# Query tiles in a PSUM bank of their own, with their products and rotary steps at other places of the map loop

## What is computed

```python
q, kc, vc, ks, vs, kw, vw, gt = jnp.split(h @ w_in, splits, axis=-1)
q = to_q_groups(apply_rope(q.reshape(b, seq, NSA_HEADS, hd), cos, sin), g)
kc = compress(kc, ...); vc = compress(vc, ...)
s_cmp = jnp.einsum('bgrqd,bgcd->bgrqc', q, kc) * scale
p_cmp = masked_softmax(s_cmp, cmask)
o_cmp = jnp.einsum('bgrqc,bgcd->bgrqd', p_cmp, vc)
...                      # o_slc: softmax over selected blocks; 8 blocks, top 16, so all causal ones
o_win = banded_attention(q, kw, vw, WIN_LEN)
o = gates[..., 0, None] * o_cmp + gates[..., 1, None] * o_slc + gates[..., 2, None] * o_win
return from_q_groups(o) @ w_o
```

## Time and profile before

| | before |
|---|---|
| three runs | 2541.85, 2544.45, 2547.47 us |
| median | 2544.45 us |
| the profiled execution | 2543.68 us, its span 2541.8 us |
| TensorE, matmuls busy | 2467.0 us, 97% |
| VectorE, ScalarE, GpSimd busy | 53%, 32%, 71% |
| mean granted TensorE clock | 0.993 of full speed |
| the loop over maps | from 126.8 us, scores of the last map at 328.5 us |

### The profile page before, as it was taken

How to read it: one execution, slowest core, us unless ns; L and a number is a source line. 1 busy time by engine, 2 the same in 40 slices (tenths; PEclk the granted TensorE clock), 3 DMA queues, 4 the chain that set the end, 5 groups by cost and what they waited for, 6 DMA issues and landing times.

```text
span 2541.8 us, 34039 instructions
## 1 busy us (share of the span) xinstructions
PE 2467.0 (97%) x11830; PEld 2064.1 (81%) x11830; DVE 1337.4 (53%) x2087; ACT 806.9 (32%) x1754; POOL 1797.6 (71%) x1589
## 2 busy tenths in 40 slices
PE   9999999999998999999999899999999999999997
PEld 7888888888887888888888777888878887788886
DVE  7778755665037656663177855343125455543312
ACT  3377742111028631110156533111015563311101
POOL 7867776676668876666699987666666668666664
PEclk9999999999999999999999999999999999999999
DMA  4300012323321123223222212233222221232232
GB/s 145 116 26 26 26 58 91 99 93 97 100 88 52 53 91 99 93 97 104 91 75 67 67 59 80 94 99 97 93 83 76 67 75 58 83 99 92 98 100 75
DMA packets 58117, 208.61 MB, mean 82 GB/s; under 512 B 6496, under 2 KB 6752, under 8 KB 58016
## 3 DMA queue, kind: packets, MB, share of 16 engines
q1 hardware_dynamic: 57744, 206.88, 24.9%
q10 hardware_dynamic: 272, 0.39, 0.1%
HBM read 205.09 MB, written 2.16 MB: 82 GB/s over the span
## 4 chain that ended last, share of the span: by engine, by line
PE 55%; POOL 5%; DVE 4%; ACT 2%; DMA 1%; issue 1%; ACTq 0%; DVEq 0%; SPq 0%; POOLq 0%
PE PS L897 17%; PE PS L899 17%; PE PS L898 17%; POOL WL L625 2%; POOL WH L623 1%; DVE PC L2860 1%; PE PS L1339 1%; ACT MP L2095 1%; DMA raw<-stream 1%; POOL RQ L692 0%; PE PS L1316 0%; POOL RQ L685 0%; PE PS L1317 0%; PE PS L1364 0%; POOL WH L622 0%
## 5 line engine op out<-in xcount | busy, mean ns | idle before, releaser
L625 POOL TENSOR_TENSOR WL<-raw,WH 128x1024 fp32r<-128x1024 f32 x380 | 921.8, 2426 | 31.7
L897 PE MATMUL PS<-HH,WH 128*128 128x512 f32 x2240 | 886.0, 396 | 20.8 <-DVE HL L2432 9.4
L899 PE MATMUL PS<-HH,WL 128*128 128x512 f32 x2240 | 876.6, 391 | 0.0
L898 PE MATMUL PS<-HL,WH 128*128 128x512 f32 x2240 | 876.2, 391 | 0.0
L897 PEld LDWEIGHTS PS<-HH,WH 128*128 128x128 f32 x2240 | 423.1, 189 | 116.4 <-issue 17.6
L899 PEld LDWEIGHTS PS<-HH,WL 128*128 128x128 f32 x2240 | 422.6, 189 | 89.4
L898 PEld LDWEIGHTS PS<-HL,WH 128*128 128x128 f32 x2240 | 423.1, 189 | 85.1 <-issue 1.0
L622 POOL TENSOR_TENSOR WH<-raw,SC 128x32 fp32r<-128x32 f32 x380 | 109.5, 288 | 490.4 <-DMA raw<-stream 475.1
L623 POOL TENSOR_SCALAR WH<-raw 128x992 fp32r<-128x992 f32 x380 | 407.2, 1072 | 0.0
L897 PE MATMUL PS<-GH,WH 128*128 (+1 forms) x688 | 268.7, 390 | 0.0
L898 PE MATMUL PS<-GL,WH 128*128 (+1 forms) x688 | 267.9, 389 | 0.0
(11 more groups left out here) (398 smaller groups left out, 3515.9 us busy)
## 6 DMA issues: line engine op xcount, KB each, us to landing
raw<-stream SPq DMA_DIRECT2D x380, 512.0 KB, 3.6
X<-x SPq DMA_DIRECT2D x4, 512.0 KB, 5.2
out<-X SPq DMA_DIRECT2D x8, 256.0 KB, 2.1
PR<-params SPq DMA_DIRECT2D x1, 536.0 KB, 8.5
spare_raw_nsa<-stream SPq DMA_DIRECT2D x1, 512.0 KB, 3.6
spare_raw_swa<-stream SPq DMA_DIRECT2D x1, 512.0 KB, 4.5
spare_raw_diff<-stream SPq DMA_DIRECT2D x1, 512.0 KB, 4.5
spare_raw_fox<-stream SPq DMA_DIRECT2D x1, 512.0 KB, 4.5
```

The lines of the kernel that those rows point to most:

```text
L625: pool.tensor_tensor(WL[:, w], raw[:, w], hi.bitcast(F32), ALU.subtract).then_inc(chunk_split, 1)
L897: pe.matmul(to, h, his[k], start=start and k == 0, stop=False)
L898: pe.matmul(to, h, los[k], start=False, stop=False)
L899: last = pe.matmul(to, l, his[k], start=False, stop=stop and k == n_k - 1)
```

## The change

For nsa, every query tile from 1 on goes to bank 6 (`Q_BANK`) and the compressed part of every pair to bank 7 (`CMP_BANK`), where tile 0 also goes. The first two output tiles go to banks 6 and 7 in that order. In pairs u from 1 on, the products of the query tiles move: at i = 0 the k-steps 2 and 3 of tile u+1 stand between the scores and the turn that waits (3 alone in pair 1), and steps 4 to 7 behind the compressed scores; nothing at i = 1; at i = 2 and i = 3 one k-step each of tile u+2, between the scores and the turn, the first of them behind a wait for the copy of tile u+1 out of the bank. In the same pairs the copy out of the bank moves from i = 1 to i = 0; the cosines to i = 1, ahead of the scaling of the compressed part; the addition to i = 1, behind the scaling of the map; first part, stacking and rest from i = 3 to i = 2. Pair 0 keeps its order. VectorE's order isn't touched. The waits for `c_lo` in `fill` at i = 3 and at m = 27 become waits for the copy.

```diff
--- before.py
+++ after.py
@@ -182,6 +182,7 @@
 TURN_BANK = (3, 4, 3)
 TURN_WIDTH = (512, 512, 256)
 AV_BANK = 5
+Q_BANK, CMP_BANK = 6, 7
 
 
 def proj_bank(x):
@@ -191,11 +192,13 @@
 
 def out_bank(kind, t):
 
-    return (proj_bank(t + 1) if kind == "nsa" else proj_bank(t)) if t < 2 else ((0, 1, 3, 2, 4, 5) if kind in GROUPED else (0, 1, 3, 2, 0, 1))[t - 2]
+    return proj_bank(t) if t < 2 else ((0, 1, 3, 2, 4, 5) if kind in GROUPED else (0, 1, 3, 2, 0, 1))[t - 2]
 
 
 def bank_at(kind, part, y=0):
 
+    if kind == "nsa" and part == "q":
+        return CMP_BANK if y == 0 else Q_BANK
     return proj_bank([x for x in ORDER[kind] if x[0] != "cmp"].index((part, y)))
 
 
@@ -835,22 +838,25 @@
                     split(c, c + 1)
                 for m in range(8 * per):
                     u, i = divmod(m, per)
+                    late = 1 if nsa and u == 0 else 0
                     if nsa and i == 0 and u < 7:
                         split(c + u, c + u + 1)
-                    if u < 7 and i == (2 if nsa else 0):
+                    if u < 7 and i == (1 + late if nsa else 0):
                         cosines(u + 1)
                     if nsa and i == cmp_step(u) + 1:
                         scale_cmp(u)
-                    if u < 7 and i == (2 if nsa else 0):
+                    if u < 7 and i == 0 and not nsa or late and i == 2:
                         if not nsa and m == 12:
                             out_rest(0)
                         add_sines(u + 1)
-                    if u < 7 and i == (3 if nsa else 1):
+                    if u < 7 and i == (2 + late if nsa else 1):
                         rest_q(u + 1, m)
                     if not nsa and i == 1 and u < 6:
                         split(c + u + 1, c + u + 2)
                     if nsa or i == 0:
                         scale(m)
+                    if nsa and 0 < u < 7 and i == 1:
+                        add_sines(u + 1)
                     for t in REST_AT[kind].get(m, ()) if nsa or m > 12 else ():
                         out_rest(t)
                     if not nsa and m == 15:
@@ -1099,7 +1105,7 @@
                     for t in range(QT):
                         for h in range(2):
                             g = 2 * (u % 2) + h
-                            to = PS[:, bank_at(kind, "q", u), 2 * (2 * t + h) * NCMP:2 * (2 * t + h + 1) * NCMP]
+                            to = PS[:, CMP_BANK, 2 * (2 * t + h) * NCMP:2 * (2 * t + h + 1) * NCMP]
                             qs = MQ[:, u % 2, h, t * P:(t + 1) * P]
                             last = pe.matmul(to, qs, KC[:, g].rearrange("p a n -> p (a n)"), start=True, stop=True)
                     last.then_inc(c_scores, 1)
@@ -1108,7 +1114,7 @@
 
                     pe.wait_ge(c_scaled, u + 1)
                     for t in range(QT):
-                        last = pe.transpose(PS[0:2 * NCMP, bank_at(kind, "q", u), t * P:(t + 1) * P],
+                        last = pe.transpose(PS[0:2 * NCMP, CMP_BANK, t * P:(t + 1) * P],
                                             CS[:, 2 * NCMP * t:2 * NCMP * (t + 1)], IDF[:])
                     last.then_inc(c_turned, 1)
 
@@ -1153,6 +1159,16 @@
                         pe.wait_ge(c_lo, u + 1)
                         pe.matmul(PS[:, AV_BANK], VC[:, k], PTC[:], start=False, stop=True).then_inc(m_av, 1)
 
+                def fill_ahead(m):
+
+                    u, i = divmod(m, per)
+                    if 0 < u < 6 and i == 2:
+                        pe.wait_ge(q_out[kind], u + 2)
+                    if 0 < u < 6 and i >= 2:
+                        proj("q", u + 2, i - 2, i - 1)
+                    if 0 < u < 7 and i == 0:
+                        proj("q", u + 1, 3 if u == 1 else 2, 4)
+
                 def fill(m):
 
                     u, i = divmod(m, per)
@@ -1176,18 +1192,13 @@
                         pe.wait_ge(mv_out, before("mv_out", kind) + 4)
                         proj("q", 1, 0, 4)
                         compress_out()
-                    elif u < 7 and i == 0:
-                        proj("q", u + 1, 3, 4)
-                    elif u < 7 and i == 1:
+                    elif u < 7 and i == (0 if u else 1):
                         proj("q", u + 1, 4, CT)
-                    elif 0 < u < 6 and i == 3:
-                        pe.wait_ge(c_lo, u + 1)
-                        proj("q", u + 2, 0, 3)
                     if u < 8 and i == cmp_step(u) + 2:
                         turn_cmp(u)
                     if m == 27:
 
-                        pe.wait_ge(c_lo, 7)
+                        pe.wait_ge(q_out[kind], 8)
                     if m == 31:
 
                         pe.wait_ge(c_lo, 8)
@@ -1253,6 +1264,8 @@
                 for m in range(8 * per + 2):
                     if m < 8 * per:
                         scores(m)
+                    if nsa:
+                        fill_ahead(m)
                     if 2 <= m < 8 * per and ng == 3:
                         turn(m - 2, (2,))
                     fill(m)
@@ -1263,6 +1276,7 @@
                     if m >= 2:
                         values(m - 2)
                     if nsa and m == 3:
+                        pe.wait_ge(q_out[kind], 2)
                         proj("q", 2, 0, 3)
                     if m == 1 and nsa:
                         pe.wait_ge(cmp_stored, 2)
@@ -1885,7 +1899,7 @@
                     act.wait_ge(c_turned, u + 1)
                     if u:
                         act.wait_ge(m_av, before("m_av", kind) + 2 * u)
-                    act.activation(PTC[0:HD], PS[0:HD, bank_at(kind, "q", u)], ACT.Copy).then_inc(c_hi, 1)
+                    act.activation(PTC[0:HD], PS[0:HD, CMP_BANK], ACT.Copy).then_inc(c_hi, 1)
 
                 def turned_first(m, gs):
 
@@ -1985,11 +2000,11 @@
                         turned_first(m - 2, (2,))
                     if m == 0 and nsa:
                         cmp_first()
-                    if nsa and i == 1 and u < 7:
+                    if nsa and i == late and u < 7:
                         evac_q(u + 1)
                     if m == cmp_step(0) + 2 and nsa:
                         turned_cmp_first(0)
-                    if nsa and i == 3 and u < 7:
+                    if nsa and i == 2 + late and u < 7:
                         stack_q(u + 1)
                     if not nsa and i == 1 and u < 6:
                         evac_q(u + 2)
@@ -2628,7 +2643,7 @@
                     if u:
                         dve.wait_ge(c_turned, u)
                     mask = MSK[:, 2].bitcast(F32).rearrange("p (t n) -> p t n", t=QT).unsqueeze(2)
-                    pairs = PS[:, bank_at(kind, "q", u)].rearrange("p (a s n) -> p a s n", s=2, n=NCMP)
+                    pairs = PS[:, CMP_BANK].rearrange("p (a s n) -> p a s n", s=2, n=NCMP)
                     own.link(dve.tensor_tensor(CS[:].rearrange("p (t h n) -> p t h n", t=QT, h=2),
                                                pairs[:, :, 0].rearrange("p (t h) n -> p t h n", h=2),
                                                mask.to_broadcast([P, QT, 2, NCMP]), ALU.add))
@@ -2652,7 +2667,7 @@
                 def turned_cmp_rest(u):
 
                     dve.wait_ge(c_hi, u + 1)
-                    dve.tensor_tensor(PTC[HD:P], PS[0:HD, bank_at(kind, "q", u)], PTC[0:HD].bitcast(F32), ALU.subtract
+                    dve.tensor_tensor(PTC[HD:P], PS[0:HD, CMP_BANK], PTC[0:HD].bitcast(F32), ALU.subtract
                                       ).then_inc(c_lo, 1)
 
                 def turned_rest(m, gs):
```

## The result

The changed kernel takes 2569.45 us (median of 4 runs, 2568.60 to 2575.61), the one before 2544.39 us: the ratio is 1.0102, 95% interval 1.0090 to 1.0114. It is 25 us slower where 23 were forecast, and inside the range of 2554 to 2578 us. Its profiled execution was its longest, 2575.61 us with a span of 2573.8; so the two profiles lie 32 us apart and not 25, and the reader should know which of the two differences a sum is for.

A forecast was written before the change was run, and what follows sets the result against it. TensorE, busy 97% of the span, was taken to lead, with VectorE setting the pace in some maps. Added to 2543.7 us, 22.8 us over pairs 1 to 6 gave 2566.5, stated as 2567; range 2554 to 2578, the forecast itself 2558 to 2573.

The forecast's parts named there:

- Map A pays in full: Map i = 0 of a pair: TensorE works throughout, so added k-steps make it 8.99 us, 3.0 longer (2.8 in pair 1).
- Map B gives nothing back: Map i = 1: shortens to about 5.5 us, but VectorE's run keeps the next turn 9.2 us after its start; no gain.
- Maps C and D a little later: Maps i = 2 and 3: moved query copies on ScalarE delay VectorE's last rest; +0.9 us a pair, 0.5 in pair 6.
- The sum: Pairs 1 to 6 together: 3.7 + 15.6 + 3.5 = 22.8 us longer, all of it reaching the kernel's end.
- Rival 4: Waits at i = 1 to 3 lower the clock, slowing the start of i = 0: 9 us more, 2576; chance 0.17.
- Rival 1: Waits at turns, bank and stack vanish in pairs 1 to 6: 2.4 us each, 14.5 faster, 2529; chance 0.11.
- Rival 2: Map i = 1 shortens by as much as i = 0 lengthens: no change that counts, near 2544 us; chance 0.05.
- Rival 3: Maps i = 2 and 3 cost nothing and might shorten by 1.3 us a pair: 2550 to 2558 us; chance 0.12.

The follow-up runs named there:

- two_in_b: rope_late with two of the six k-steps at i = 0 moved to i = 1, and the copy out of the bank back at i = 1; 2555.60 us.
- second execution: The changed kernel, unaltered, run again for a second profile; 2574.21 us, ratio 1.0119 to the kernel before.
- rope_late: Changed kernel with the next query's cosines, addition, first part, stacking and rest back at their old places, products left moved; 2562.94 us.
- spread_ahead: Against the kernel before: own bank, one k-step ahead of the turn at i = 0 and i = 3, four kept at i = 1; 2547.19 us.
- early_tile_stack: Kernel before with new banks, tile 2's first three k-steps ahead of pair 0's i = 3 values, first stacking copy ahead of exponentials; 2540.61 us.

## Why the prediction was right

**Map A pays in full: right.** 8.99 us were forecast, 9.00 are measured at full clock; pair 1, 8.3 forecast (5.53 and 2.8), 8.30 measured. two_in_b gives the price again from the other side, 0.69 us a k-step.

**Map B gives nothing back: right.** 5.5 us forecast, 5.42 to 5.44 measured, while the turn in C stands where it stood. VectorE in order of time, changed kernel, pair 3:

```profile
227.38 1.08 DVE L2619 TENSOR_REDUCE NM<-PS 128x1 f32<-128x256 f32 x3
...
233.08 1.29 DVE L2678 TENSOR_TENSOR GTL<-PS,GTH 128x512 fp32r<-128x512 f32 x2
...
235.64 0.43 DVE L2678 TENSOR_TENSOR GTL<-PS,GTH 128x256 fp32r<-128x256 f32 x1 [0.94 <-ACT GTH L1911]
...
240.26 0.69 DVE L2678 TENSOR_TENSOR GTL<-PS,GTH 128x512 fp32r<-128x512 f32 x1 [1.40 <-ACT GTH L1911]
...
243.30 0.41 DVE L2678 TENSOR_TENSOR GTL<-PS,GTH 128x256 fp32r<-128x256 f32 x1
```

Its maxima of B begin 2.60 us after B's start (2.64 in the earlier trace rows) and its rests end at 234.37, 9.59 after it (9.63 before): VectorE's run through B is unchanged, and has only been moved.

**Maps C and D a little later: right, 0.1 too large.** The steps of the walk, as us after B's start (224.78), forecast and measured, from these rows and the following of ScalarE and GpSimd:

```profile
234.71 0.63 ACT L1820 ACTIVATE WK<-WK 128x512 fp32r<-128x512 f32 x1 [2.79 <-POOL WK L818]
235.24 0.37 ACT L1911 ACTIVATE GTH<-PS 128x256 fp32r<-128x256 f32 x1
...
238.48 0.63 ACT L1824 ACTIVATE MQ<-WK 64x512 fp32r<-64x512 f32 x1
...
239.66 0.57 ACT L1911 ACTIVATE GTH<-PS 128x512 fp32r<-128x512 f32 x1
```
```profile
230.96 2.48 POOL L790 TENSOR_SCALAR GP<-GP,RR 128x128 f32<-128x128 f32 x4
233.41 1.26 POOL L818 TENSOR_TENSOR WK<-WK 128x512 f32<-128x512 f32 x1
...
239.03 2.05 POOL L790 TENSOR_SCALAR GP<-GP,RR 128x128 f32<-128x128 f32 x4 [1.02 <-DVE RR L2634]
```

| step | forecast | measured |
|---|---|---|
| GpSimd's addition ends | 10.0 | 9.89 |
| copy of the last turned group in C | 10.6 | 10.46 |
| copy of the next turned group | 15.0 | 14.88 |
| scaling of C ends | 16.4 | 16.30 |
| last rest in D written | 19.1 | 18.93 |
| next pair, at full clock | 20.5 | 20.37 |

The last is from the second execution. Before it was 19.58, so the way from B to the next pair grew by 0.79 us and not 0.9. rope_late, at 19.56, shows that this is the price of the moved query steps and of nothing else.

**The sum.** At full clock the pairs are 28.7, four times 29.4 and 29.4 us where they were 25.09, 25.54 and 25.90: 3.6 + 4 x 3.8 + 3.5 = 22.3 us against 22.8 forecast. One figure of the working was off without bearing on the sum: the split of the next weights ends 5.0 us into A, not 6.4.

**What was not in the sum.** Rival 4, the falling clock, was given 0.17 and happened in part: 1.4 us for each pair it hits, twice in one execution and four times in the other, so 3 to 6 us. With it 22.3 become 25 to 28, and the medians of the two sets lie at 25 and 29 over the kernel before. In the first profile the loop up to pair 7 is 29.6 us longer: 22.3 for the order of work, 5.8 for the clock in pairs 2 to 6, 1.4 for pair 0, where the low clock came in C before and came in D after; some 2.4 us lie outside the loop. That the rival and the forecast could both hold, the rival in some pairs only, was the weak place of my cases: I treated it as all six pairs or none. Its size per pair was about right (1.5 us), its working was not: it had TensorE waiting some 7 us of a pair, and busy for 1.2 of the 4 us before D's values are through; measured are 4.4 us, and 2.12 of 4 in the row above. It also put the loss at the start of A, and most of it is in D. It is in part luck that the number came this close. The sum had nothing for the clock; the first set lies 2.4 us above the 2567 forecast, and the second set of the same kernel, 2574.21 us, lies 7 above it. That is inside the whole range, but just outside the 2558 to 2573 given to the forecast itself.

**The other rivals.** Rival 1 needed VectorE's rests 1.8 us into B; the values got the one they lacked at 2.7 and the last at 4.1 (227.51 and 228.84 above). spread_ahead tested its core, products ahead of two of the three waiting turns with B left as it was, and found no gain. The row that spoke against it, VectorE's unbroken run, was the one to believe; its busy share of a pair fell from 80% to 69% (20.40 of 29.37 us), as forecast. Rival 2 needed B to shorten by what A grew: A grew by 3.0 us, B shortened by 1.5, and C took more than that back (7.06 for 5.01). Rival 3 supposed that without the two copies in the way a pair could be 1.3 us shorter from B on; rope_late shows that putting both back where they were gives the old 19.6 and no less, because the second stacking copy then ends last. No run here came near 18.2 us from B to the next pair; the shortest is 18.95, in early_tile_stack, by moving a copy and not by this change.

## What to carry to other kernels

An engine that is busy 97% of the time can still be waiting for others in some steps of a loop and be the bound in others. Filler is free only in the first kind, so before spreading it evenly read each step's length against the chain of the other engines. Here 0.69 us of products cost 0.69 us in one map and 0.05 in the next. A wait that shows on the busiest engine need not be lost time: filling two of them (spread_ahead) won nothing, while one 0.63 us copy moved on an engine that is busy 74% of a pair won 0.63 us a pair, as that copy stood in the chain that closes the loop. The same move cost 1.3 us in pair 0, where that engine had no pause, and by itself it was not enough to be told from no change over the whole kernel.

## What was not expected of the hardware

The granted clock is a part of the time that a schedule can't be read off for: the same program had it fall in four pairs in one execution and in two in the next, each 1.2 us in D and 0.2 to 0.3 in the map behind, in the case shown above after 4 us in which TensorE was busy for 2.1. With thirteen useless products a pair no fall came in the one profiled execution, and they cost no time; that they prevent the falls is not shown. The same holds for pair 0. In the eight profiles of kernels that do the same in it, this one's before and after among them, it lasted 28.05 to 29.65 us by where the low clock came, while VectorE's rest of the compressed part ended 24.8 us after the loop's start in every one: a spread of 1.6 us from one profile to another, more than some of the edits moved.
